# Two-layer decoder trunk on one core: both parts of x kept in natural order, memory products spread over four expert pairs, a scatter placed later

## The reference

```python
# cross-attention: keys and values come from the memory tokens alone
k = (mem @ w_xk).reshape(bn, m_len, XATTN_HEADS, XATTN_HEAD_DIM)
v = (mem @ w_xv).reshape(bn, m_len, XATTN_HEADS, XATTN_HEAD_DIM)
...
# mixture of experts: 64 experts, each token uses 8 of them
hid = jax.nn.silu(jnp.einsum('btd,edf->btef', xt, w_gate)) * jnp.einsum('btd,edf->btef', xt, w_up)
return jnp.einsum('btef,efd->btd', hid * gt[..., None], w_down)
...
x = layer_norm(DEEPNORM_ALPHA * x + ffn, ln3_g[l], ln3_b[l])
```

## Time and profile before

| | us |
|---|---|
| median of 3 executions | 1642.58 (1642.04 to 1642.69) |
| the profiled execution, its own time | 1642.27 |
| its span | 1640.5 |
| TensorE busy | 1595.4 |
| VectorE, ScalarE, GpSimd busy | 387.3, 301.1, 80.4 |
| expert part of layer 0, first gates to last scatter | 375.8 to 841.7 |
| expert part of layer 1 | 1177.4 to 1628.5 |

### The profile page before, as it was taken

One profiled execution on the slowest core, in us unless ns is written; L12 is line 12 of the kernel. 1 busy time (PEld: TensorE's weight loads), 2 busy tenths in 40 slices (PEclk: granted clock), 3 DMA queues, 4 the chain that ended last, 5 costly groups with the idle time before them and its releaser, 6 DMA issues.

```text
span 1640.5 us, 19683 instructions
## 1 busy us (share of the span) xinstructions
PE 1595.4 (97%) x7997; PEld 894.4 (55%) x7997; DVE 387.3 (24%) x825; ACT 301.1 (18%) x600; POOL 80.4 (5%) x92
## 2 busy tenths in 40 slices
PE   8999999999999999999999999999999999998995
PEld 6878868574333353333358788685733333333331
DVE  1222221052222111222221232212521222222213
ACT  1022011022212111112120230121321122211211
POOL 2000020030000000000020000201200000000000
PEclk9999999999999999999999999999999999999998
DMA  9246444459999999999992463435799999999995
GB/s 347 85 166 244 144 148 151 180 212 369 420 408 421 421 413 389 421 420 418 414 392 104 148 237 128 154 141 201 298 422 421 421 421 421 421 421 421 421 412 240
DMA packets 113516, 509.96 MB, mean 311 GB/s; under 512 B 8451, under 2 KB 16773, under 8 KB 70933
## 3 DMA queue, kind: packets, MB, share of 16 engines
q1 hardware_dynamic: 112864, 508.59, 77.8%
q0 software_dynamic: 224, 0.12, 0.0%
q10 hardware_dynamic: 340, 0.02, 0.0%
HBM read 507.64 MB, written 1.05 MB: 310 GB/s over the span
## 4 chain that ended last, share of the span: by engine, by line
PE 84%; SPq 8%; DMA 5%; DVE 2%; issue 1%; ACT 1%; DVEq 0%
PE work L805 40%; PE work L1240 21%; PE work L1279 11%; SPq L603 8%; DMA arena<-in_w_up 4%; PE moe_sum L1184 4%; PE work L1135 3%; PE moe_sum L1111 1%; PE work L1264 1%; PE moe_sum L1176 1%; PE work L1142 0%; DMA ring<-in_w_xk 0%; PE work L852 0%; PE work L958 0%; PE work L981 0%
## 5 line engine op out<-in xcount | busy, mean ns | idle before, releaser
L1240 PE MATMUL work<-ring,arena 128*64 128x512 f32 x1472 | 341.1, 596 | 6.7 <-DMA ring<-in_w_up 6.7
L805 PE MATMUL work<-XT,ring 128*128 128x256 f32 (+1 forms) x1408 | 280.3, 360 | 1.3 <-DVE arena L1811 1.3
L805 PEld LDWEIGHTS work<-XT,ring 128*128 128x128 f32 x1408 | 247.5, 190 | 32.6 <-issue 3.0
L1240 PEld LDWEIGHTS work<-ring,arena 128*64 128x64 f32 x1472 | 109.1, 137 | 215.6 <-issue 207.0
L1279 PE MATMUL work<-ring,hidden 128*64 128x512 f32 x736 | 168.1, 599 | 2.1 <-DVE hidden L2020 2.1
L1240 PE MATMUL work<-arena 128*64 128x512 f32 x576 | 141.6, 594 | 4.8 <-DMA arena<-in_w_up 4.5
L2027 DVE TENSOR_TENSOR out_lo<-work,out_hi 128x512 fp32r<-128x512 f32 x128 | 88.5, 692 | 231.0 <-ACT out_hi L1550 231.0
L805 PE MATMUL work<-ring,arena 128*128 128x512 f32 (+1 forms) x336 | 140.4, 577 | 0.0
L2016 DVE SCALAR_TENSOR_TENSOR hidden<-hidden,slot_gate,work 128x256 f32<-128x256 f32 x64 | 30.8, 480 | 423.4 <-ACT hidden L1544 423.4
L1550 ACT CAST out_hi<-work 128x512 fp32r<-128x512 f32 x128 | 75.2, 587 | 236.2 <-PE work L1279 236.2
L1544 ACT ACTIVATE hidden<-work 128x256 f32<-128x256 f32 x64 | 24.6, 384 | 432.0 <-PE work L1240 432.0
(11 more groups left out here) (226 smaller groups left out, 1288.1 us busy)
## 6 DMA issues: line engine op xcount, KB each, us to landing
ring<-in_w_gate SPq DMA_DIRECT2D x92, 1024.0 KB, 14.9
ring<-in_w_up SPq DMA_DIRECT2D x92, 1024.0 KB, 17.0
ring<-in_w_down SPq DMA_DIRECT2D x92, 1024.0 KB, 15.7
arena<-in_w_down SPq DMA_DIRECT2D x36, 1024.0 KB, 16.1
arena<-in_w_gate SPq DMA_DIRECT2D x36, 1024.0 KB, 14.6
arena<-in_w_up SPq DMA_DIRECT2D x36, 1024.0 KB, 16.7
ring<-in_w_in SPq DMA_DIRECT2D x28, 1024.0 KB, 12.7
ring<-in_w_mix_out SPq DMA_DIRECT2D x8, 1024.0 KB, 12.9
```

The source lines that it names most:

```text
L805: mm = pe.matmul(dst, a, b, start=(k == 0), stop=(k == len(pairs) - 1))
L1240: mm = pe.matmul(work[0][rows, :], gathered_pair(b, c, k)[:, rows], w, start=(c == 0), stop=(c == KC - 1))
```

## The change

It does four things.

- **x in natural order.** `round_input` and the subtraction on GpSimd copy x as it lies. The gather's weights become `part[:, t, c::KC]`, 128 elements with a step of 8; `add_input` reads 512 elements side by side. The helpers `in_chunks`, `in_rows` and `by_chunk` go.
- **The memory products** leave their place before body 2. `memory_ahead(job)` makes one of the four in each pair of body 2's second batch (pairs 20 to 23 of the layer), after the straight scatter and before the wait for `hid`, in bank 3. SyncE loads the two memory units as the 62nd and 69th unit of the layer's stream (`AHEAD_ORDER`; before they were the 48th and 49th), in places of `ring`. ScalarE copies each product between its silu and its casts of the same pair.
- **The looped body's loads.** Two of the places that the looped body fills first are now those of the memory units. Its fourth load waits for the last memory product (`held`), and so does all behind it in SyncE's order.
- **The banks of `gather_first`** become 3, 0, 2, 3, 0, 2, 3, 1, and the transposes of `sel_gate` go to bank 1. The scatter of the last pair (`between`) comes after the second chunk of gathers.

The core of the diff:

```diff
-AHEAD_AT = 2
-AHEAD_UNITS = 2
+AHEAD_BODY = LONG_BODIES - 1
+AHEAD_ORDER = (62, 69)
+AHEAD_UNITS = len(AHEAD_ORDER)
...
-FIRST_BANKS = (3, 1, 2)
+FIRST_BANKS = (3, 0, 2, 3, 0, 2, 3, 1)
+GATE_BANK = 1
...
                     for m in range(UNITS * RING_USES):
-                        wait_unit_read(m, pairs, halves)
+                        n = LONG_BODIES * 3 * BODY_PAIRS + (AHEAD_UNITS if l < DEPTH - 1 else 0) + m - UNITS
+                        held = l < DEPTH - 1 and n in AHEAD_ORDER
+                        if held:
+                            alone(sp, memory_filled, 2 * AHEAD_UNITS)
+                        last = m if held else max(m, UNITS + unit_at(l, n) - LONG_BODIES * 3 * BODY_PAIRS)
+                        wait_unit_read(last if m < UNITS else m, pairs, halves)
                         load_unit(m, pair_firsts[m // 3])
...
                 for j in range(LONG_BODIES):
-                    if j == AHEAD_AT and l < DEPTH - 1:
-                        load_ahead(0, w_xk)
-                        load_ahead(1, w_xv)
                     for m in range(0 if j else LONG, UNITS * RING_USES):
+                        if l < DEPTH - 1 and order_of(l, j, m) - 1 in AHEAD_ORDER:
+                            i = AHEAD_ORDER.index(order_of(l, j, m) - 1)
+                            load_ahead(i, (w_xk, w_xv)[i])
                         wait_place_read(l, order_of(l, j, m), base)
                         load_unit(m, firsts(j)[m // 3], j)
...
-                    pool.tensor_tensor(by_chunk(x_lo, t), in_chunks(X, t), by_chunk(x_hi, t).bitcast(F32),
+                    pool.tensor_tensor(x_lo[:, t, :], X[:, t, :], x_hi[:, t, :].bitcast(F32),
                                        ALU.subtract).then_inc(x_split_ready, 1)
...
-                            mm = pe.matmul(dst[:, :, t, :], part[:, t, c * P:(c + 1) * P], src,
+                            mm = pe.matmul(dst[:, :, t, :], part[:, t, c::KC], src,
                                            start=(part is x_hi), stop=(part is x_lo))
...
                     for c in range(KC):
-                        if c >= 3:
+                        if FIRST_BANKS[c] == GATE_BANK:
+                            pe.wait_ge(gated_ready, snap(pe, batch + 1))
+                        elif c >= 3:
                             pe.wait_ge(gather_ready[(c - 3) % 2], snap(pe, batch * (KC // 2) + ((c - 3) // 2 + 1)))
-                        gather(c, FIRST_BANKS[c % 3])
-                        if c == 0 and between:
+                        gather(c, FIRST_BANKS[c])
+                        if c == 1 and between:
                             between()
                         if c == 1:
                             pe.wait_ge(sel_gate_ready, snap(pe, batch + (l + 1)))
-                            transpose_gated(0)
-                    pe.wait_ge(gated_ready, snap(pe, batch + 1))
+                            transpose_gated(GATE_BANK)
+                    last = max(c for c in range(KC) if FIRST_BANKS[c] == 0)
+                    pe.wait_ge(gather_ready[last % 2], snap(pe, batch * (KC // 2) + (last // 2 + 1)))
...
-                        rows = in_rows(part, t)[:, half * (BANK // KC):(half + 1) * (BANK // KC), :]
-                        pe.matmul(moe_sum[i][:, :].rearrange("p (q c) -> p q c", c=KC), ident_r[:, :], rows,
+                        pe.matmul(moe_sum[i][:, :], ident_r[:, :], part[:, t, half * BANK:(half + 1) * BANK],
                                   start=False, stop=False, skip_group_check=True)
...
+                def memory_ahead(job):
+
+                    i, part = job // 2, job % 2
+                    u, n = in_ring(l, AHEAD_ORDER[i]), uses_of(l, AHEAD_ORDER[i])
+                    pe.wait_ge(slot_loaded[u], ((DENSE_USES if u < RING else DEPTH) + n) * 32)
+                    weights = unit[u].rearrange("p (k n) -> p k n", k=KC)
+                    if job:
+                        pe.wait_ge(memory_taken, job)
+                    else:
+                        pe.wait_ge(gather_ready[0], ((AHEAD_BODY + 1) * 2) * (KC // 2))
...
+                        if l < DEPTH - 1 and j == AHEAD_BODY and b == 1:
+                            memory_ahead(k)
...
-                    act.copy(by_chunk(x_hi, t), in_chunks(X, t)).then_inc(x_hi_ready, 1)
+                    act.copy(x_hi[:, t, :], X[:, t, :]).then_inc(x_hi_ready, 1)
...
+                        if l < DEPTH - 1 and j == AHEAD_BODY and b == 1:
+                            take_memory(k)
```

More of the change, by code:

```diff
@@ L413, in order_of, with unit_at @@
             n = j * 3 * BODY_PAIRS + m
-            return n + AHEAD_UNITS if l < DEPTH - 1 and j >= AHEAD_AT else n
-        def ahead_order(i):
-            return AHEAD_AT * 3 * BODY_PAIRS + i
+            if l < DEPTH - 1:
+                for at in AHEAD_ORDER:
+                    n += n >= at
+            return n
+        def unit_at(l, n):
+            return n - sum(at < n for at in AHEAD_ORDER) if l < DEPTH - 1 else n
         def uses_of(l, n):
@@ L553, in wait_place_read @@
                 last = max(i for i in range(n) if in_ring(l, i) == in_ring(l, n))
[L554 to L560, removed]
+                if l < DEPTH - 1 and last in AHEAD_ORDER:
+                    alone(sp, memory_filled, 2 * AHEAD_ORDER.index(last) + 2)
+                    return
+                q, part = divmod(unit_at(l, last), 3)
                 if part == 2:
@@ L1199, in scatter_crossed @@
                     scatter(b, k, ((2, 0), (3, 0), (0, 1), (1, 1))).then_inc(scattered, 1)
+                def memory_ahead(job):
[7 more added lines that the diff above has]
+                        pe.wait_ge(gather_ready[0], ((AHEAD_BODY + 1) * 2) * (KC // 2))
+                    if i == 0:
+                        for m in range(2):
+                            cols = slice((2 * part + m) * P, (2 * part + m + 1) * P)
+                            mm = accumulate(work[3][:, m * SEQ:(m + 1) * SEQ],
+                                            [(weights[:, c, cols], memT[:, c, :]) for c in range(KC)])
+                    else:
+                        mm = accumulate(work[3][:, :], [(memT[:, c, part * P:(part + 1) * P], weights[:, c, :])
+                                                        for c in range(KC)])
+                    mm.then_inc(memory_filled, 1)
                 def expert_body(body, j=None):
+                    if j is None and l < DEPTH - 1:
+                        pe.wait_ge(memory_taken, 2 * AHEAD_UNITS)
                     loaded = [snap(pe, units_used(u, l, base, body, j) * 32) for u in (0, RING, UNITS)]
@@ L1288, in expert_body @@
                             add_input(q - (BODY_PAIRS - 4))
-                def memory_ahead():
-                    weights = []
-                    for i in range(AHEAD_UNITS):
-                        u, n = in_ring(l, ahead_order(i)), uses_of(l, ahead_order(i))
-                        credit = DENSE_USES if u < RING else DEPTH
-                        pe.wait_ge(slot_loaded[u], (credit + n) * 32)
-                        weights.append(unit[u].rearrange("p (k n) -> p k n", k=KC))
-                        for part in range(2):
-                            bank = (0, 3)[part]
-                            if i == 0 and bank == 3:
-                                pe.wait_ge(gather_ready[0], (base + AHEAD_AT) * 2 * (KC // 2) + KC // 2)
-                            if i == 1:
-                                pe.wait_ge(memory_taken, part + 1)
-                            if i == 0:
-                                for m in range(2):
-                                    cols = slice((2 * part + m) * P, (2 * part + m + 1) * P)
-                                    mm = accumulate(work[bank][:, m * SEQ:(m + 1) * SEQ],
-                                                    [(weights[0][:, c, cols], memT[:, c, :]) for c in range(KC)])
-                            else:
-                                mm = accumulate(work[bank][:, :],
-                                                [(memT[:, c, part * P:(part + 1) * P], weights[1][:, c, :])
-                                                 for c in range(KC)])
-                            mm.then_inc(memory_filled, 1)
-                    pe.wait_ge(memory_taken, 2 * AHEAD_UNITS - 1)
                 for j in range(LONG_BODIES):
-                    if j == AHEAD_AT and l < DEPTH - 1:
-                        memory_ahead()
                     expert_body(snap(pe, base + j), j)
@@ L1557, in _ @@
                     expert_body(act.snap(base + i), 0)
-                if l < DEPTH - 1:
-                    for i in range(2 * AHEAD_UNITS):
-                        act.wait_ge(memory_filled, i + 1)
-                        w = work[(0, 3)[i % 2]][:, :]
-                        if i < 2:
-                            ins = act.copy(xkT[:, KC // 2 + 2 * i:KC // 2 + 2 * i + 2, :],
-                                           w.rearrange("p (m t) -> p m t", m=2))
-                        else:
```

(2 more changed lines are left out.)

24 lines of the change are left out of this document (12 added, 12 removed).

## The result

| | before | after |
|---|---|---|
| median of 6 executions, us | 1642.49 (1642.04 to 1642.99) | 1676.74 (1676.12 to 1678.04) |
| the profiled execution, us | 1642.27 | 1677.77 |
| its span, us | 1640.5 | 1676.0 |

The ratio is 1.0211, with a 95% interval from 1.0200 to 1.0221: the changed kernel is **slower by 34 us**. The forecast was 1641.1 us, within a range from 1638.5 to 1644.0. What came about is rival B, and stronger than B was priced (1666 us).

What follows compares the result with a forecast made beforehand. Layer 0 was taken as bound by TensorE, layer 1 by transfers. Only the memory products counted: 0.7 + 0.8 = 1.5 us off 1642.58 gives 1641.1 us, range 1638.5 to 1644.0; natural order and layer 1's gains counted 0.

Steps and rivals of the forecast that it cites:

- rival B: Gathers not hidden by waits: stepped weight loads slow each by 0.097 us, giving 1666 us (mild form 1643.7); chance 0.10.
- part 2: x in natural order: `add_input` saves 2.9 us a layer, eaten by waits; stepped gather loads and unstepped casts cost or gain nothing.
- Sum: Gathers: stepped load and product no longer overlap, 0.22 us a matmul; the prediction's other end, 0.097 us more.
- Part 1, the memory products: Moved into pairs 20 to 23, the products of 6.94 us make layer 0 1.5 us shorter (0.8 to 2.0).
- 19.2 and 26.4: Layer 0: us for a pair with a memory product, and from pair 23 to the gates of pair 24.
- dry queue: Layer 0 near 721 us: SyncE's load waits for the last memory product, transfers run dry for 0 to 2 us, without loss.
- vanished wait of 0.84 us: End of layer 0: the last pair's wait for its second half goes, as the stream regains up to 3.1 us; counted 0.8.
- new waits for weights: Layer 0 before pair 21: TensorE waits 3 to 5 us in all, including 2.9 us of `add_input` savings lost there.
- Part 2, `add_input`: Pairs 4 to 7: unstepped 512-column matmul takes 0.24 us instead of 0.60, saving 2.9 us a layer, counted as 0.
- Part 3, the later scatter: Looped body's head: scatter one chunk of gathers later, so the 0.8 us wait before it shrinks by 0.5 us.
- Rival A: TensorE alone decides: weights of pair 20 there by 645 us, all savings count, 5.8 us, 1636.8 us; chance 0.12.
- rival C: SyncE's new wait costs over 3 us of stream at 721 us; layer 0 loses its gain: 1642.6 or 1-2 us more; chance 0.13.

Runs made afterwards that it cites:

- e8: Changed kernel with its gathers replaced by fp32 transposes of x at a step of 8, 128 identity columns: 1638.18 us.
- e5: Changed kernel with gathers at a step of 8 multiplying 128 identity columns instead of 256 of `sel`, fp32r: 1691.48 us.
- e7: Changed kernel with gathers as plain fp32 matmuls, step 8, 128 identity columns, two records each: 1796.06 us.
- e2: Changed kernel with x in chunks again (unstepped weights, stepped `add_input`), memory products and later scatter kept: 1640.86 us, ratio 0.9995 to the kernel before.
- e4: Changed kernel with x in runs of 2 features, weights 8 bytes apart: 1640.96 us, ratio 0.9996.
- e9: Changed kernel with gather weights at a step of 3 elements, so other columns of x are gathered: 1649.72 us in one execution.
- e3: Changed kernel with x in runs of 4 features, weights 16 bytes apart: 1674.30 us, ratio 1.0196.
- e1: Kernel before with only x in natural order (gather weights at a step of 8, `add_input` unstepped): 1679.97 us, ratio 1.0237.
- e6: Changed kernel with gathers on unstepped weights, multiplying 128 identity columns instead of 256 of `sel`, fp32r: 1640.88 us.

## Why the prediction was wrong, point by point

**The step that failed** is the last of part 2: "A load is there every 0.111 us at worst, below the gather's 0.121, so I cost the step at 0." The 0.111 was read from the stepped transposes of L852 and carried over to the loads of a matmul. e8 (the transposes) shows that the reading was right for transposes, e5 and e7 (step 8 with half the columns, in fp32r and fp32) that it does not hold for matmuls. In its place, a stepped load takes 0.242 us and the gathers follow it. The runs in one table (*lines* are those of 16 bytes that a load touches):

| weights | step | lines | load, ns | apart, us |
|---|---|---|---|---|
| gather, 256 columns (before, e2) | 1 | 32 | 189 | 0.121 |
| gather (e4) | 2 | 64 | 196 | 0.121 |
| gather (e9) | 3 | 96 | 265 | 0.177 |
| gather (e3) | 4 | 128 | 332 | 0.236 |
| gather (after, e1) | 8 | 128 | 338 | 0.242 |
| fp32r matmul, 128 columns (e6) | 1 | 32 | 192 | 0.11 |
| fp32r matmul, 128 columns (e5) | 8 | 128 | 336 | 0.240 |
| fp32 matmul, 128 columns (e7) | 8 | 128 | 335 | 0.238 |
| fp32 transpose, 128 columns (e8) | 8 | 128 | 193 | 0.111 |

Rule and row stood against each other there. The Trainium skill's lines of 16 bytes said that each load would be slower, the pace of the transposes said not, and I followed the pace. The row would have deserved the preference had it shown the same operation. The text even had the hint: the transposes' load grew from 141 to 192 ns with the step, and the gather's unstepped load already took 189. So the records of the two operations are not to be measured by one scale. What the rule lacked was the size. The prediction's own sign of being wrong, gathers over 0.13 us apart, is what came.

**Rival B** had the mechanism and the places right, at a chance of 0.10, with two terms too small. Its price, 0.097 us, was built on *Sum*, which e5 refutes; measured are 0.121. And it took the gathers of layer 1 behind its first gates as hidden, but they cost 9.1 us. How much of new work a stage can hide is read from the windows of the whole stage: layer 0 from its first gates to the `memT` product behind it, layer 1 from its first gates to the end (columns as in the earlier trace rows). Before:

```profile
375.80:841.70 465.90, 458.42 (x2470) 185.44 (x2469) 94.22 (x173) 84.50 (x160) 0.00 (x0) 1.00 1.00 411
1177.40:1640.50 463.10, 434.14 (x2372) 168.78 (x2372) 102.58 (x190) 83.61 (x158) 1.10 (x2) 0.98 0.97 401
```

After:

```profile
377.20:863.80 486.60, 482.60 (x2470) 213.03 (x2469) 94.33 (x173) 86.73 (x159) 0.00 (x0) 1.00 0.98 398
1203.80:1676.00 472.20, 455.05 (x2372) 194.65 (x2372) 102.70 (x190) 85.83 (x157) 1.10 (x2) 0.99 0.95 392
```

The first number after the comma is TensorE's busy time; stage less busy is its idle time. In layer 0 the idle time fell from 7.5 to 4.0 us: 3.5 us of cover. In layer 1 it fell from 29.0 to 17.2 us: 11.8 us of cover, of which 10.6 were waits for weights; no wait for a transfer is left in it. The gathers bring 224 x 0.121 = 27.1 us to each, `add_input` takes 2.2 back. In layer 1 the busy time grew by 20.9 us only; of the 4.0 us that are missing, 2.3 lie in the gate and up matmuls (the mean of the larger group fell from 599 to 593 ns, and one stretch of before, 1460 to 1470 us, had a granted clock of 0.83), the rest was not followed.

With a smaller price the same cover does more. Three kernels share the placement:

| | extra per gather, us | layer 0 longer by | layer 1 longer by |
|---|---|---|---|
| e9 against e2 | 0.056 (12.5 in 224) | 5.5 | 1.1 |
| after against e2 | 0.121 (27.1 in 224) | 20.4 | 9.0 |

(466.15, 471.65 and 486.58 us in layer 0; 463.2, 464.3 and 472.2 in layer 1.) At 0.056 us the transfers of layer 1 hide nearly everything, and TensorE still waits 5.6 us for weights there; at 0.121 the cover is used up, and what exceeds it shows. A slack is an amount, not a yes or no.

**Part 1, the memory products**: right in its pieces, with e2 and e4 as witnesses, since their gathers are as quick as before. 19.08 and 26.27 us against 19.2 and 26.4; the dry queue of 2.3 us against 0 to 2; the vanished wait of 0.84 us at the end. The new waits for weights, 3.4 us in e2 and 1.5 in e4, are no witness for the forecast of 3 to 5, whose main term neither kernel has. In the changed kernel itself a pair with a product also takes 19.1 us (685.82 to 704.93), as no gathers lie in it. The gain of layer 0 was put at 1.5 us, from 0.8 to 2.0. Between the profiled executions it is -0.2 us in e2 (466.15 against 465.91) and 1.7 in e4 (464.25). The difference lies in pair 20, whose gates start 274.6 us after the first gates in e2 and 272.6 in e4; the forecast had 272.3, and said that a late stream would eat the gain. One place where e2's stream fell behind is the window from 480 to 490 us, with 355 GB/s against e4's 397. By their medians both kernels are 0.2 to 0.3 us under the one before. The sum without the failed step is thus not contradicted, but both intervals hold a gain of 1.5 us as well as none, so it is not confirmed either.

**Part 2, `add_input`**: 0.33 us for 512 unstepped columns instead of my 0.24, so 2.2 us in a layer instead of 2.9. The 0.24 was twice the 0.121 us of a gather of 256 columns read in runs of 32, and 512 unstepped columns take 2.7 times that. It had been counted as 0 because the waits eat it; now that TensorE is the bound it counts, and pays back 4.4 of 62 us.

**Part 2, the casts**: ScalarE's copy of x fell from 2061 to 1033 ns and GpSimd's subtraction from 2854 to 2356 (medians), in natural order. As forecast, it brought nothing, since they are over before the gathers start.

**Part 3, the later scatter**: the wait before it went from 0.8 to 0.3 us in e2, as forecast, and to nothing in the changed kernel, where the gathers ahead of it last longer. Parts 1 and 3 together are worth 488.74 - 486.58 = 2.2 us in layer 0 (e1 against after) where TensorE is the bound, against 1.6 + 0.5 forecast. **Rival A**'s condition, that TensorE alone decides, thus holds in the slow kernels and only there; **rival C**'s dry queue came, and cost nothing.

No kernel that computes the whole result beat the one before by more than the measurement can tell. With quick gathers layer 1 is held by its transfers, and the most that any run shows for parts 1 and 3 in layer 0 is 2.2 us.

## What to carry to other kernels

Before a layout is changed so that weights are read with a step, count the 16-byte lines that a load touches: in this kernel a step of two fp32 elements was free, at a step of four or eight a load of 128 columns took 0.24 us with 256 moving columns as with 128, and the gathers took twice their time. A measured pace overrides a rule only when it is the pace of the same operation; if it is a relative's, it shows little, and a rule that speaks against it deserves the larger chance, since nothing here was to be gained that could pay for it (2 x 2.2 us against 62). And a layout has a reader and a writer: the side that runs 256 times a layer is the one to keep contiguous, as the kernel before does.

## What was unexpected of the hardware

- The fp32 transposes of TensorE are exempt: at a step of 8 elements they keep 0.111 us and a load record of 193 ns, where matmuls on the same operand need 0.240 us and 336 ns.
- The price of a matmul's load goes by lines, in proportion from 96 on: 0.177 us at 96 lines, 0.236 to 0.242 at 128, and hardly more for lines that lie further apart (step 4 against 8). At 32 lines it is 0.11, not 0.06.
- The moving operand behaves otherwise. The two `add_input` matmuls of 512 columns take 1.20 us at a step of 128 elements (before), 1.13 in runs of 2 (e4), 0.70 in runs of 4 (e3) and 0.66 side by side (after). Runs of 8 bytes, free for weights, gain almost nothing there; runs of 16 bytes gain nearly all.
- In e5 and in one product of the changed kernel the granted clock fell for a while (window means of 0.93 and 0.67), though TensorE was 99% busy or more in e5's windows. In e6 it was 0.66 from 375 to 380 us, and the first gates took 8.71 us instead of 7.02. The kernel before has 0.83 from 1460 to 1470 us, in a window where TensorE was busy for 7.9 of 10 us. Why it fell in the busy stretches stays unexplained.
